# The second attention's queries and keys projected and normed by token, and turned by VectorE and GpSimd's transfers

## The chip, the core and the metric

The kernel runs on one core of a Trainium2 chip. The core's engines have a queue each and run side by side: TensorE (PE: matrix products into PSUM; PEld is its weight load), VectorE (DVE) and ScalarE (ACT) for arithmetic, GpSimd (POOL) and SyncE (SP), which here only issue transfers. ScalarE can issue transfers too. Engines wait for one another by semaphores. The metric is the time of one execution in device microseconds; a lower one is better.

## What is computed

One token block of 256 tokens and width 2048 goes through a pooling mixer with a gated residual, then through a gated DeltaNet layer and a banded attention. All is in float32. The change touches the attention alone (its inputs, cut to what matters):

```
proj = h @ w_in                                  # 256 x 2048 times 2048 x 8192: q, k, v, z
q = rms_norm_2(q by head, q_norm_w)              # 16 heads of 128
k = rms_norm_2(k by head, k_norm_w)
s = q . k * 128**-0.5 + bias                     # bias by distance, band of 9 chunks of 64, causal by chunk
p = softmax(s)
o = (p . v) * silu(z)
out = h + o @ w_out

rms_norm_2(x, w) = x * rsqrt(mean(x*x over the head's 128) + 1e-6) * w
```

## The kernel before

**Projections.** Every large product streams the weights once from DRAM, in 392 slabs of 512 KB (`raw`, four slots). ScalarE rounds a slab to its high part `w_hi` (`hi_parts`), VectorE subtracts for the low part `w_lo` (`lo_parts`), both in eight slots, and TensorE multiplies high by high, high by low and low by high. A group is 512 output columns over all 2048 inputs: eight slabs, one call of `group` or `joined`. ScalarE and VectorE convert slabs from 15 on behind the group's first (`AHEAD = 15`); a slot is free when TensorE has counted up `s_used`. Results go to `acc`, two halves of PSUM used in turn; `s_free` says that VectorE or ScalarE has read one.

**Two orders of a product.** `joined` has the channels on the partitions of the result: it holds a 128×128 piece of weights and streams the operand `b_op` (all 256 tokens, high and low part side by side) past it, 512 columns for the high weights (line 751) and 256 for the low ones (line 753), 64 such pairs a group. It delivers half a group at a time (two units of `acc`). `by_token` (lines 694 to 696) holds the tokens and streams 512 columns of weights, 96 products a group; its result has the tokens on the partitions and channels along the row.

**A round of the attention** takes four heads: groups q, k, v, z (`G_B + 4 i`, ...), then the next four heads, in all four rounds. q, k and z are joined, v is by token. For q and k, ScalarE copies the low part of the result (`low_half`), VectorE adds the high part and multiplies by the root of the token's norm (`evicted_half`), ScalarE squares, the squares are split in a high and a low part (`sq_hi`, `sq_lo`), and TensorE sums them over a head's channels by a product with ones (`split_sums`: four heads, two products each, 128×256), put between two slabs of k and of v. ScalarE then makes the inverse root (`rsqrt`: a logarithm and an exponential, each with a load of its table), VectorE scales by root and norm weight. Since q (`t2`) and k (`t0`) have channels on the partitions, TensorE can multiply them at once: `scores(i)`, put behind slab 6 of v (fillers are called behind a slab of that number, counted from 0).

**Behind the scores**: VectorE adds the bias (`t4`, loaded by GpSimd), masks, takes the maximum; ScalarE exponentiates; VectorE normalises and transposes 32×32 squares inside `p_t` into `p_tt`. The squares themselves change places on a trip through DRAM, issued by ScalarE between its slabs: one write `p_d<-p_tt`, a wait for it, and four reads `p_tt<-p_d` of 32 partitions each, in pieces of 128 B (lines 1604 and 1610). `attended(i)` multiplies with v behind slab 2 of the next q group, or, for the last round, of the first output group.

Every engine's order is the order in which the code is written; no scheduler moves anything. GpSimd's queue is in order too: a transfer behind a wait stays behind it.

## Time and profile before

| | us |
|---|---|
| median of 3 runs (1363.56 to 1366.82) | 1364.05 |
| the profiled execution | 1362.52 |
| its span, first to last instruction | 1360.7 |
| TensorE busy | 1349.9 |
| VectorE busy | 991.2 |
| ScalarE busy | 748.9 |

Busy time is a share of the span and says nothing yet of what waits. A TensorE instruction's row is longer than the distance to the next one, since products overlap; its price is the distance between two starts. The page's slices are 34 us each.

### The profile page before, as it was taken

The numbers are of one execution on the slowest core, as the hardware profiler recorded it, in microseconds if no ns is written. First come the engines' busy times: TensorE is split into PE (matmuls) and PEld (weight loads), VectorE is DVE, ScalarE is ACT, GpSimd is POOL, SyncE is SP. The second block draws the span as 40 slices with busy tenths as digits, with TensorE's granted clock in tenths as the row PEclk, the third lists the DMA queues.
The fourth block names the chain that finished last, engine by engine and source line by source line (L and its number), as shares of the span: only waits on it lengthen the run. The fifth ranks groups of instructions, "written<-read, shape, count | busy, mean of one in ns | idle before, by whom it ended". The sixth has DMA issues, their size and how long they took to land.

```text
span 1360.7 us, 20324 instructions
## 1 busy us (share of the span) xinstructions
PE 1349.9 (99%) x7759; PEld 1149.8 (85%) x7759; DVE 991.2 (73%) x1287; ACT 748.9 (55%) x984; POOL 51.4 (4%) x102
## 2 busy tenths in 40 slices
PE   8999999999999999999999999999999999999999
PEld 4445999988888888888999988888888888888887
DVE  3568989977679999899677677765666566666652
ACT  2214445555766566546788765466476566466431
POOL 0000022000001000010000000000000000000000
PEclk9999999999999999999999999999999999999999
DMA  9999999856476666474645756555755756755752
GB/s 383 414 417 382 346 375 409 302 198 202 159 268 212 223 240 221 170 271 158 201 144 167 225 189 218 192 164 185 206 197 186 203 198 202 201 186 183 222 197 80
DMA packets 105670, 316.30 MB, mean 232 GB/s; under 512 B 33952, under 2 KB 34352, under 8 KB 101104
## 3 DMA queue, kind: packets, MB, share of 16 engines
q1 hardware_dynamic: 67824, 261.30, 55.2%
q0 software_dynamic: 12352, 47.50, 9.7%
q10 hardware_dynamic: 25408, 6.29, 2.2%
q8 instruction: 61, 1.00, 0.3%
q14 instruction: 25, 0.20, 0.0%
HBM read 299.31 MB, written 17.84 MB: 233 GB/s over the span
## 4 chain that ended last, share of the span: by engine, by line
PE 90%; DVE 5%; DMA 3%; issue 1%; SPq 1%; ACT 0%; DVEq 0%; ACTq 0%
PE acc L751 40%; PE acc L753 20%; PE misc L776 3%; PE acc L776 3%; PE misc L1006 3%; PE acc L695 2%; PE acc L694 2%; PE acc L696 2%; DVE w_lo L1665 2%; PE acc L683 2%; PE acc L685 2%; PE acc L686 2%; DMA mod_ring<-mod_w 2%; DMA u_ring<-weights 1%; PE misc L686 1%; PE misc L685 1%
## 5 line engine op out<-in xcount | busy, mean ns | idle before, releaser
L751 PE MATMUL acc<-b_op,w_hi 128*128 128x512 f32 x1792 | 633.3, 398 | 2.1 <-DVE vo L1709 2.1
L1665 DVE TENSOR_TENSOR w_lo<-raw,w_hi 128x1024 fp32r<-128x1024 f32 x392 | 469.8, 1221 | 192.0 <-ACT w_hi L1177 188.1
L1177 ACT ACTIVATE w_hi<-raw 128x1024 fp32r<-128x1024 f32 x392 | 403.7, 1053 | 265.9 <-DMA raw<-weights 116.3
L753 PE MATMUL acc<-b_op,w_lo 128*128 128x256 f32 x1792 | 500.9, 280 | 0.0
L751 PEld LDWEIGHTS acc<-b_op,w_hi 128*128 128x128 f32 x1792 | 336.6, 188 | 80.0 <-DVE vo L1709 2.4
L753 PEld LDWEIGHTS acc<-b_op,w_lo 128*128 128x128 f32 x1792 | 338.2, 189 | 0.3
L751 PE MATMUL acc<-a_op,w_hi 128*128 128x512 f32 x760 | 266.7, 396 | 0.0
L753 PE MATMUL acc<-a_op,w_lo 128*128 128x256 f32 x760 | 212.5, 280 | 0.0
L751 PEld LDWEIGHTS acc<-a_op,w_hi 128*128 128x128 f32 x760 | 142.6, 188 | 33.5 <-DVEq L2132 0.2
L753 PEld LDWEIGHTS acc<-a_op,w_lo 128*128 128x128 f32 x760 | 143.5, 189 | 0.1
L1635 DVE CUSTOM_DVE_ANT_0 mod_ring<-mod_ring,silu_b,vecs 128x2048 f32<-128x2048 f32 x26 | 61.1, 2350 | 46.5 <-DMA mod_ring<-mod_w 46.5
L776 PE MATMUL acc<-u_ring,vo 128*128 128x512 f32 x128 | 57.9, 596 | 4.3 <-ACT vo L1210 2.6
L776 PE MATMUL misc<-u_ring,vo 128*128 128x512 f32 x128 | 57.5, 592 | 0.0
L776 PEld LDWEIGHTS acc<-u_ring,vo 128*128 128x128 f32 x128 | 23.9, 190 | 35.8 <-issue 30.1
L694 PE MATMUL acc<-w_hi,b_op 128*128 128x512 f32 x128 | 50.2, 392 | 0.0
L695 PE MATMUL acc<-w_lo,b_op 128*128 128x512 f32 x128 | 49.9, 390 | 0.0
L696 PE MATMUL acc<-w_hi,b_op 128*128 128x512 f32 x128 | 49.9, 390 | 0.0
L776 PEld LDWEIGHTS misc<-u_ring,vo 128*128 128x128 f32 x128 | 24.3, 190 | 30.1 <-issue 29.9
L1210 ACT ACTIVATE vo<-xres,modv 128x256 f32<-128x256 f32 x16 | 8.1, 508 | 63.8 <-DVE modv L1635 63.8
L1941 DVE SCALAR_TENSOR_TENSOR t<-t,vecs,t 128x255 f32<-128x255 f32 (+2 forms) x96 | 38.9, 478 | 1.9 <-ACT t L1349 1.9
L1006 PE MATMUL misc<-t,t 128*128 128x128 f32 x320 | 38.4, 275 | 0.0
L1006 PEld LDWEIGHTS misc<-t,t 128*128 128x128 f32 x320 | 37.1, 192 | 0.9 <-issue 0.2
(275 smaller groups left out, 1675.1 us busy)
## 6 DMA issues: line engine op xcount, KB each, us to landing
raw<-weights SPq DMA_DIRECT2D x392, 512.0 KB, 4.4
mod_ring<-mod_w SPq DMA_DIRECT2D x26, 1024.0 KB, 12.7
u_ring<-weights SPq DMA_DIRECT2D x32, 512.0 KB, 11.9
gate_ring<-weights POOLq DMA_DIRECT2D x30, 512.0 KB, 8.6
mod_late<-mod_w SPq DMA_DIRECT2D x6, 1024.0 KB, 7.8
p_d<-p_tt ACTq DMA_DIRECT2D x4, 768.0 KB, 3.5
p_tt<-p_d ACTq DMA_DIRECT2D x16, 192.0 KB, 8.0
xres<-x_t SPq DMA_DIRECT2D x4, 512.0 KB, 16.1
```

The lines of the kernel that those rows point to most:

```text
L685: nc.tensor.matmul(to, wh[:, ch], xl, start=False, stop=False, skip_group_check=True)
L686: last = nc.tensor.matmul(to, wl[:, ch], xh, start=False, stop=end and m % 2 == 1, skip_group_check=True)
L694: nc.tensor.matmul(to, xh[:, t], wh, start=kt == 0, stop=False)
L695: nc.tensor.matmul(to, xh[:, t], wl, start=False, stop=False)
L696: last = nc.tensor.matmul(to, xl[:, t], wh, start=False, stop=end)
L751: nc.tensor.matmul(to, w_hi[:, slot, ch], op[:, kt], start=kt == 0, stop=False, skip_group_check=True)
L753: last = nc.tensor.matmul(to[:, 0:T], w_lo[:, slot, ch], op[:, kt, 0:T], start=False, stop=kt == KT - 1, skip_group_check=True)
L776: last = nc.tensor.matmul(bank(2 * j + half), vo[:, kt, half * P:(half + 1) * P], u_ring[:, 2 * (kt % 4) + j // 2, j % 2 * GC:(j % 2 + 1) ...
L1006: last = nc.tensor.matmul(misc[:, k:k + P], tile_of(lhs, half, h), tile_of(rhs, half, h), start=True, stop=True)
L1177: nc.scalar.activation(w_hi[:, m.c % HL_SLOTS], raw[:, q.c % RAW_SLOTS], ACT.Copy).then_inc(own.up(s_hi), 1)
L1635: nc.vector.tensor_tensor_reduce(out=tile, in0=tile, in1=weight, scale=1.0, scalar=start, op0=ALU.mult, op1=ALU.add, accum_out=out).then_i ...
L1665: nc.vector.tensor_tensor(w_lo[:, slot], raw[:, q.c % RAW_SLOTS], w_hi[:, slot].bitcast(F32), ALU.subtract).then_inc(own.up(s_lo), 1)
```

## The change

- q and k are projected by token, as v. The stream of weights is laid out for that (`slabs(m, [q, k, v])`). A round now has five units of `acc` in place of seven.
- Head by head, ScalarE squares the result straight from `acc` with an accumulated sum along the row (`head_squares`), then takes logarithm and exponential of 128×8 numbers. The token's own root is not multiplied in; instead the epsilon is divided by its square (`eps_tok`). VectorE scales head by head with root and norm weight (`head_rows`, loaded once by GpSimd) and transposes 32×32 squares.
- `split_sums` and the splitting of the squares are gone.
- The squares of q, of k and of the probabilities change places by `turned`, on GpSimd's queue: four writes to DRAM in pieces of 512 B, a wait, four reads in pieces of 128 B. ScalarE issues no transfers any more.
- The scores wait for the transfers of q and k (`s_head_t`) and stand behind the last slab of v (slab 7); the attended products stand behind slab 3.

```diff
@@ gpsimd
+            pool.dma_start(head_rows[:], rows_d.to_broadcast([P, 2 * P])).then_inc(s_rows, 16)
...
+            def turned(tile, through, ready, n, written, done):
+
+                pool.wait_ge(ready, n)
+                for a in range(4):
+                    rows = tile[32 * a:32 * a + 32].rearrange("p (n c) -> p n c", c=P)
+                    pool.dma_start(through[:, :, a], rows).then_inc(written, 16)
+                pool.wait_ge(written, 64 * n)
+                for b in range(4):
+                    squares_of = through.rearrange("x n a c -> x (n a) c")[:, :, 32 * b:32 * b + 32]
+                    pool.dma_start(tile[32 * b:32 * b + 32].rearrange("p (k t) -> p k t", t=32), squares_of
+                                   ).then_inc(done, 16)
+
+            pool.wait_ge(s_x1, 5)
+            pool.wait_ge(s_bx, 16)
+            bias_rows(0)
+            for i in range(4):
+                for k, tile in enumerate((t2[:], t0[:, 0:BATCH * T])):
+                    turned(tile, head_d[k], s_head_32, 2 * i + k + 1, s_head_d, s_head_t)
+                if i < 3:
+                    pool.wait_ge(s_biased, i + 1)
+                    bias_rows(i + 1)
+                turned(p_tt[:], p_d, s_turned, i + 1, s_p_d, s_p_tt)
@@ tensor
             def scores(i):
 
-                pe.wait_ge(s_bn, turn(2, i, 2).v)
+                pe.wait_ge(s_head_t, turn(128, i, 128).v)
...
-            joined(G_B, b_op, ready=lambda kt: O_AO + kt + 1, fillers={3: last_sums_b, 6: root_by_token},
-                   order=SPLIT)
+            tokens(G_B, ready=lambda kt: O_AO + kt + 1, fillers={3: last_sums_b, 6: root_by_token})
             for i in range(4):
+                g = G_B + 4 * i
                 if i:
-                    joined(G_B + 4 * i, b_op, fillers={2: lambda: attended(i - 1)})
-                key_value_gate(i)
+                    tokens(g, fillers={3: lambda: attended(i - 1)})
+                tokens(g + 1)
+                tokens(g + 2, fillers={7: lambda: scores(i)})
+                joined(g + 3, b_op)
@@ scalar
+            def head_squares(par, power):
+
+                for half in range(2):
+                    for h in range(BATCH):
+                        k = half * GC + h * P
+                        nc.scalar.activation(squares_b[:, k:k + P], acc[:, par, k:k + P], ACT.Square,
+                                             accum_out=head_sums[:, h, half:half + 1]
+                                             ).then_inc(own.up(s_sq2), 1)
+                act.wait_ge(*own.last())
+                act.wait_ge(s_etok, 1)
+                for half in range(2):
+                    nc.scalar.activation(head_roots[:, :, half], head_sums[:, :, half], ACT.Ln,
+                                         bias=eps_tok[:, half:half + 1], scale=1.0 / P).then_inc(own.up(s_act), 1)
+                act.wait_ge(*own.last())
+                nc.scalar.activation(head_roots[:], head_roots[:], ACT.Exp, bias=power, scale=-0.5
+                                     ).then_inc(own.up(s_rinv), 1)
...
-                act.wait_ge(s_turned, Num(1, i, 1).v)
-                act.dma_start(p_d, p_tt[:]).then_inc(s_p_d, 16)
-                hi_parts(n + 4, 3)
-                act.wait_ge(s_p_d, Num(16, i, 16).v)
-                for b in range(4):
-                    of = bass.AP(tensor=p_d.tensor, offset=p_d.offset + 32 * b,
-                                 ap=[[PAIRS, 32], [P, PAIRS // P], [32 * PAIRS, 4], [1, 32]])
-                    act.dma_start(p_tt[32 * b:32 * b + 32].rearrange("p (n a t) -> p n a t", a=4, t=32), of
-                                  ).then_inc(s_p_tt, 16)
-                hi_parts(n + 7, 1)
+                hi_parts(n + 4, 4)
@@ vector
-                    evicted_half(g, 1, r1, s_qs)
-                    dve.wait_ge(s_sqh, Num(1 + k, i, 2).v)
-                    nc.vector.tensor_tensor(sq_lo[:], t1[:, 0:4 * T], sq_hi[:].bitcast(F32), ALU.subtract
-                                            ).then_inc(own.up(s_sql), 1)
...
                     dve.wait_ge(s_rinv, Num(5 + k, i, 2).v)
...
-                    scaled(out[:, 0:4 * T], src[:, 0:4 * T], vecs[:, w:w + 1], t3[:], done=s_bn)
+                    for half in range(2):
+                        for h in range(BATCH):
+                            at_ = h * T + half * P
+                            scaled(t3[:, at_:at_ + P], acc[:, unit_of(g) % 2, half * GC + h * P:half * GC + (h + 1) * P],
+                                   head_roots[:, h, half:half + 1], head_rows[:, k * P:(k + 1) * P])
+                    dve.wait_ge(*own.last())
+                    dve.sem_inc(own.also(s_free), 1)
+                    if i:
+                        dve.wait_ge(s_score, i)
+                    nc.vector.transpose(out[:, 0:BATCH * T], t3[:]).then_inc(own.up(s_head_32), 1)
+                    lo_parts(n, SLABS)
```

ScalarE in the first round, from the end of the key group to the value group, before (`t_57` is `t1`, `t_59` is `t3`, `small` the constants):

```order
L1202 ACTIVATE k_s<-acc 128x512 [waits s_used]
L1573 ACTIVATE t_57<-k_s 128x1024 [waits s_qs,s_bn]
L1575 ACTIVATE sq_hi<-t_57 128x1024 [waits s_sq2]
...
L1195 ACT_TABLE_LOAD
L1195 ACTIVATE t_59<-misc,small 128x1024 [waits s_nrm]
L1197 ACT_TABLE_LOAD
L1197 ACTIVATE t_59<-t_59 128x1024 [waits s_act]
...
L1588 ACTIVATE v_n<-acc,r_tok 128x512 [waits s_rtok,s_used]
```

and now:

```order
L1579 ACTIVATE squares_b,head_sums<-acc 128x128 [waits s_head_32,s_used]
L1579 ACTIVATE squares_b,head_sums<-acc 128x128 x7
L1585 ACT_TABLE_LOAD [waits s_etok]
L1585 ACTIVATE head_roots<-head_sums,eps_tok 128x4 [waits s_sq2]
L1585 ACTIVATE head_roots<-head_sums,eps_tok 128x4
L1588 ACT_TABLE_LOAD
L1588 ACTIVATE head_roots<-head_roots 128x8 [waits s_act]
...
L1606 ACTIVATE v_n<-acc,r_tok 128x512 [waits s_rtok,s_used]
```

The wait for TensorE's sums (`s_nrm`) is gone; the squares, roots and both table loads now stand in one piece behind the group's end.

GpSimd in the first two rounds, before (`t_60` is `t4`):

```order
L665 DMA xres<-x_d 128x4096 [waits s_solve_pe]
L672 DMA t_60<-bias_x 128x1024 [waits s_bx,s_x1]
L672 DMA t_60<-bias_x 128x1024 [waits s_biased] x3
```

and now (`t_58` is q, `t_56` is k; 256x1x128 are 256 pieces of 128 numbers, 32x32x32 are 1024 pieces of 32):

```order
L673 DMA t_60<-bias_x 128x1024
L680 DMA head_d<-t_58 256x1x128 x4
L684 DMA t_58<-head_d 32x32x32 x4
L680 DMA head_d<-t_56 256x1x128 x4
L684 DMA t_56<-head_d 32x32x32 x4
L673 DMA t_60<-bias_x 128x1024
L680 DMA p_d<-p_tt 384x1x128 x4
L684 DMA p_tt<-p_d 32x48x32 x4
```

Where GpSimd issued one transfer a round, it now issues 25, each trip's reads behind the landing of its writes.

TensorE around the scores of the first round, before:

```order
L695 MATMUL acc<-w_lo,b_op 128x512
L696 MATMUL acc<-w_hi,b_op 128x512
L1113 MATMUL misc<-t_56,t_58 128x256
L1115 MATMUL misc<-t_56,t_58 128x128
...
L694 MATMUL acc<-w_hi,b_op 128x512
...
L751 MATMUL acc<-b_op,w_hi 128x512
L753 MATMUL acc<-b_op,w_lo 128x256
```

and now:

```order
L719 MATMUL acc<-w_lo,b_op 128x512
L720 MATMUL acc<-w_hi,b_op 128x512
L1127 MATMUL misc<-t_56,t_58 128x256
L1129 MATMUL misc<-t_56,t_58 128x128
...
L775 MATMUL acc<-b_op,w_hi 128x512
L777 MATMUL acc<-b_op,w_lo 128x256
```

One slab of v (12 products) stood between the scores and the gate group z; now the scores are followed by z at once.

## Rows read from the trace of the kernel before

**Rows 1.** The page: TensorE's share, and its granted clock in 40 slices.

```profile
PE 1349.9 (99%) x7759; PEld 1149.8 (85%) x7759; DVE 991.2 (73%) x1287; ACT 748.9 (55%) x984; POOL 51.4 (4%) x102
...
PEclk9999999999999999999999999999999999999999
```

**Rows 2.** TensorE's waits (total us, times, longest), first and last of four.

```profile
PE acc L776 <- ACT vo L1210: 2.6, 2, 1.4
...
PE misc L820 <- DVE r L1763: 1.2, 1, 1.2
```

**Rows 3.** TensorE's instructions by time: start us, us, line, out<-in, shapes.

```profile
940.21 0.29 PE L928 MATMUL misc<-sq_hi,ones_r 128*128 128x256 f32 x1
...
941.17 0.39 PE L694 MATMUL acc<-w_hi,b_op 128*128 128x512 f32 x1
...
949.36 0.59 PE L1113 MATMUL misc<-t,t 128*128 128x256 f32 x2
...
951.89 0.48 PE L694 MATMUL acc<-w_hi,b_op 128*128 128x512 f32 x1
...
954.71 0.39 PE L751 MATMUL acc<-b_op,w_hi 128*128 128x512 f32 x1
...
985.79 0.38 PE L1125 MATMUL misc<-p_tt,v_n 128*128 128x128 f32 x2
...
988.39 0.47 PE L751 MATMUL acc<-b_op,w_hi 128*128 128x512 f32 x1
...
1013.44 0.28 PE L928 MATMUL misc<-sq_hi,ones_r 128*128 128x256 f32 x1
...
1045.52 0.59 PE L1113 MATMUL misc<-t,t 128*128 128x256 f32 x2
```

**Rows 4.** ScalarE by time: a table load, the value eviction, exponentials of 128 columns.

```profile
938.83 1.28 ACT L1195 ACT_TABLE_LOAD   x1
...
954.91 1.27 ACT L1588 ACTIVATE v_n<-acc,r_tok 128x512 f32<-128x512 f32 x2 [4.24 <-PE acc L696]
...
961.10 0.39 ACT L1597 ACTIVATE p_t<-p_t,row_max 128x128 f32<-128x128 f32 x1
961.40 0.19 ACT L1597 ACTIVATION_READ_ACCUMULATOR p_t<-p_t,row_max 128x1 f32 x1
961.49 0.39 ACT L1597 ACTIVATE p_t<-p_t,row_max 128x128 f32<-128x128 f32 x1
```

**Rows 5.** VectorE: scalings and transposes, by time, and one group (busy, mean ns).

```profile
565.73 2.69 DVE L1699 SCALAR_TENSOR_TENSOR l_t<-misc,beta,dec_t 128x256 f32<-128x256 f32 x8
...
L2098 DVE STREAM_TRANSPOSE blk<-l_c 128x1024 f32<-128x1024 f32 x1 | 2.1, 2114 | 0.0
...
966.58 1.78 DVE L2284 STREAM_TRANSPOSE p_tt<-p_t 128x1536 f32<-128x1536 f32 x1
```

**Rows 6.** GpSimd's issues by line: count, busy us, mean ns, idle before them.

```profile
L587 POOL DMA_DIRECT2D gate_ring<-weights x30 | 15.8, 528 | 199.5 <-PE acc L776 76.8 <-DVE t L1699 53.9 <-DVE gate_half L1635 41.7
...
L661 POOL DMA_DIRECT2D bias_x<-bias x1 | 1.1, 1068 | 0.0
```

**Rows 7.** DMA issues: count, KB each, median us from issue to landing.

```profile
p_tt<-p_d ACTq DMA_DIRECT2D x16, 192.0 KB, 8.0
...
l_d<-l_t POOLq DMA_DIRECT2D x4, 512.0 KB, 3.0
...
bias_x<-bias POOLq DMA_DIRECT2D x1, 2048.0 KB, 15.5
...
t<-bias_x POOLq DMA_DIRECT2D x4, 512.0 KB, 4.2
```

**Rows 8.** ScalarE's queue by time: the four reads of the first round.

```profile
971.95 10.30 ACTq L1610 DMA_DIRECT2D p_tt<-p_d  x4
```

**Rows 9.** Busy time by stretch; the last columns are PEclk, DMA share, GB/s.

```profile
882.90:1265.80 382.90, 382.90 (x2129) 332.52 (x2128) 241.05 (x243) 230.23 (x289) 1.58 (x3) 1.00 0.61 193
974.00:984.00 10.00, 10.00 (x58) 8.67 (x57) 0.87 (x2) 1.62 (x3) 0.00 (x0) 1.00 0.92 215
```

More of the change, by code:

```diff
@@ L165, in low_of @@
     i, k = divmod(g - G_B, 4)
-    return 2 * (G_AOUT - G_A) + 6 * i + (0, 2, None, 4)[k] + h + 1
+    return 2 * (G_AOUT - G_A) + 2 * i + h + 1
 def first_half(g):
-    return slab_of(Num(g)).c + (7 if g in (G_WOUT, G_A, G_AOUT, G_B, G_BOUT) else 4)
+    return slab_of(Num(g)).c + (7 if g in (G_WOUT, G_A, G_AOUT, G_BOUT) else 4)
 def slab_of(g):
@@ L207, in mod_before, with program @@
     return max(k for k in range(i) if MOD_SLOT[k] == MOD_SLOT[i])
-def program(nc, weights, mod_w, x_t, c_d, vecs_d, consts_d, window_d, w_ab_d, bias_d, out_d):
+def program(nc, weights, mod_w, x_t, c_d, vecs_d, consts_d, window_d, w_ab_d, bias_d, rows_d, out_d):
     ctx = ExitStack()
@@ L348, in half_to @@
             if g >= G_B:
-                return half_of((t0, k_s, None, t1)[(g - G_B) % 4], h)
+                return half_of(t1, h)
             if c < 8:
@@ L359, in program @@
         x_d = nc.dram_tensor("x_d", (P, KT, T), F32).ap()
-        p_d = nc.dram_tensor("p_d", (P, PAIRS), F32).ap()
+        p_d = nc.dram_tensor("p_d", (32, PAIRS // P, 4, P), F32).ap()
+        head_d = [nc.dram_tensor(f"head{k}_d", (32, 2 * BATCH, 4, P), F32).ap() for k in range(2)]
         query_d = nc.dram_tensor("query_d", (P, HEADS * T), F32).ap()
@@ L920, in last_out_sums @@
                 last.then_inc(s_nrm, 1)
-            def split_sums(n):
-                pe.wait_ge(s_ones, 1)
-                pe.wait_ge(s_sql, n.v)
-                for h in range(BATCH):
-                    out, of = misc[:, h * T:(h + 1) * T], slice(h * T, (h + 1) * T)
-                    nc.tensor.matmul(out, ones_r[:], sq_hi[:, of], start=True, stop=False)
-                    last = nc.tensor.matmul(out, ones_r[:], sq_lo[:, of], start=False, stop=True)
-                last.then_inc(s_nrm, 1)
             def key_products(i, q, done):
@@ L1131, in attended, with tokens @@
                 last.then_inc(s_pv, 1)
-            def key_value_gate(i):
-                g = G_B + 4 * i + 1
-                joined(g, b_op, fillers={3: lambda: split_sums(turn(1, i, 2))})
-                u = unit_of(g + 1)
-                group(Num(u - 1), slab_of(Num(g + 1)), u % 2, 0, b_hi, b_lo, products=by_token, fillers={
-                    3: lambda: split_sums(turn(2, i, 2)), 6: lambda: scores(i)})
-                joined(g + 2, b_op)
-            joined(G_B, b_op, ready=lambda kt: O_AO + kt + 1, fillers={3: last_sums_b, 6: root_by_token},
-                   order=SPLIT)
+            def tokens(g, **more):
+                u = unit_of(g)
+                group(Num(u - 1), slab_of(Num(g)), u % 2, 0, b_hi, b_lo, products=by_token, **more)
+            tokens(G_B, ready=lambda kt: O_AO + kt + 1, fillers={3: last_sums_b, 6: root_by_token})
             for i in range(4):
+                g = G_B + 4 * i
                 if i:
-                    joined(G_B + 4 * i, b_op, fillers={2: lambda: attended(i - 1)})
-                key_value_gate(i)
+                    tokens(g, fillers={3: lambda: attended(i - 1)})
+                tokens(g + 1)
+                tokens(g + 2, fillers={7: lambda: scores(i)})
+                joined(g + 3, b_op)
             for j in range(4):
                 joined(G_BOUT + j, a_op, ready=None if j else lambda kt: O_B + kt // 4 + 1,
-                       fillers=None if j else {2: lambda: attended(3)}, order=PLAIN if j else SPLIT)
+                       fillers=None if j else {3: lambda: attended(3)}, order=PLAIN if j else SPLIT)
             last_slab()
@@ L2360, in build_stream @@
         q, k, v, z = (D * part + GC * j for part in range(4))
-        b += [joined_slabs(m, q, PLAIN if j else SPLIT), joined_slabs(m, k), slabs(m, [v]), joined_slabs(m, z)]
+        b += [slabs(m, [q, k, v]), joined_slabs(m, z)]
     rest = np.concatenate([g, grp, joined_stage(i["pool_w_out"][0], quarters), joined_stage(a, order_a),
@@ L2419 @@
         "bias": rel[:, ::-1],
+        "rows": np.concatenate([i["b_q_norm_w_2"], i["b_k_norm_w_2"]], axis=1),
     }
```

78 lines of the change are left out of this document (31 added, 47 removed).

## The prediction

> **What bounds the kernel now.** I read four views, in this order. The page first: TensorE is busy 99% of the span, and its granted clock is full, the 2.4 GHz level, from the first slice to the last [rows 1]. Then TensorE's waits: four groups in the whole span, the largest a few microseconds, and none after 880 us, so in the whole second attention nothing is ever waited for [rows 2]. Third, TensorE's instructions by time, to price its own work. Last, ScalarE, VectorE, GpSimd and the DMA issues, to price the new chain beside it. A kernel of this kind gets faster by exactly what TensorE no longer does, and slower by every microsecond for which it is made to wait. The second attention lasts from 882.9 to 1265.8 us, 382.9 us, four rounds of 96.16 us (scores at 949.36, again at 1045.52) [rows 3, 9].
>
> **TensorE's own work.** Removed: eight blocks of sums of squares. One block is 941.17 − 940.21 = 0.96 us [rows 3], so 8 × 0.96 = 7.7 us. Changed: eight groups (queries and keys, four times) go from joined to by-token order. Both orders stream the same columns (64 × 768 = 96 × 512). By token, the 36 matmuls from 941.17 to 949.36 take 8.19 us, 0.2275 each, so a group of 96 is 21.8 us. Joined, 88 pairs take 985.79 − 954.71 = 31.08 us (0.353 each, 22.6 a group) and the 72 pairs behind the attended products take 1013.44 − 988.39 = 25.05 us (0.348, 22.3 a group) [rows 3]. A converted group is thus worth 0.3 to 0.8 us. The slower pace runs from the scores to the attended products; some pace like it will stay there, so I take 0.4: 3.3 us. Scores and attended products keep their shapes. Sum: −11.0 us, between −10.0 and −14.0 (all eight groups at 0.8).
>
> **The chain to the scores.** Today the key chain has three quarters of the value group before it. Now it starts when the key group ends (call this E) and the scores stand behind the value group's last slab, at E + 21.8. What lies between:
> - TensorE to ScalarE 0.2 (954.71 to 954.91). Eight squares with an accumulated sum of 128 columns: the exponentials of that width follow each other by 961.49 − 961.10 = 0.39, so 3.1. Then two activations on 4 columns and one on 8, about 0.2 each (the shortest ScalarE row there, an accumulator read, takes 0.19), and a table load of 1.28 before the logarithm and one before the exponential, as today [rows 4]. Together 6.5.
> - VectorE: eight scalings of 128×128. Eight of width 256 and 128 mixed take 2.69, so 2.3. The transpose has 1024 columns: 1.78 × 1024/1536 = 1.2; the other 1024-column transposes take 2.1, but they permute, so 1.2 is the nearer one [rows 5]. With semaphores the first GpSimd transfer can be issued at E + 10.4 (bounds 9.9 and 11.9).
> - So the round trip of the keys has 11.4 us. The queries' trip starts 21.8 us earlier and is out of the way if it takes under 21.8.
>
> **The round trip itself**, nowhere in the trace of before in this form. It is four writes of 256 pieces of 512 B, a wait, then four reads of 1024 pieces of 128 B. GpSimd issues a DMA of 128 pieces in 0.53 us and the one of 16×128 = 2048 pieces (bias_x) in 1.07 [rows 6]: (1.07 − 0.53)/1920 = 0.3 ns a piece. The issue alone is then 4 × 0.6 for the writes and 4 × 0.8 = 3.2 for the reads. Writes: the last is issued at 1.8; a GpSimd write of 512 KB lands in 3.0, a quarter of it hardly earlier than 2.5, so they have landed after 4.3 to 5.0. Reads: GpSimd's plain 512 KB read lands in 4.2 [rows 7], a floor of about 5 with the pieces; the same kind of read from ScalarE's queue took 10.3 us to issue for 6144 pieces, 1.7 ns a piece, with the DMA engines 92% busy from 974 to 984 [rows 8, 9]; with about 2 for the last landing (estimate) 12.4, so 4096 pieces take 12.4 × 2/3 = 8.3 at that pace. Round trip: 9.3 to 13.3 us, against a room of 11.4. I take 11.5, about the middle, since the engines' share in this stretch leaves room (0.61) but the weights are no longer held back by a blocked ScalarE. That is late by 0.1; with some scatter on a wait that can't be negative I put 0.3 a round, in all **+1.2 us**. Bounds of this term: 0, and 1.9 + 1.5 (the late start above) = 3.4 a round, 13.6 in all.
>
> **The probabilities' trip.** Now on GpSimd behind the next bias rows (one more issue of 0.53, waited for by nobody until the next round). From the end of the scores (951.89) to the end of the transpose (966.58 + 1.78) are 16.5 us [rows 3, 5]; scores that come one slab later find ScalarE's slab of that moment already done, about 2 less, 14.5. The trip has 6144 pieces: writes 5, reads at most 12.4, so it is ready at 31.9 after the scores. The attended products now stand behind 64 pairs and four slabs by token, 22.6 + 10.9 = 33.5. Slack 1.6: hidden, and 0.4 late in the bad corner (16.5 instead of 14.5). Take 0.
>
> **What else moves.** ScalarE loses its DMA issues with the 10.3 us block [rows 8], the copies, the large squares, logarithms and exponentials; VectorE loses eight half evictions and the subtractions. None is waited for, so I count nothing. Converted weights reach seven slabs (19 us) ahead; the two engines now spend 6.5 and 10 us in a row at a group's end, covered by that. The fourth attended products sit one slab later in the first output group; their operand is needed two slabs (5.5 us) behind, and the multiply, the copy and the subtraction take about 1.2 + 1.1 + 1.2 + semaphores, 4 us: covered by 1.5. The small load of norm rows on GpSimd is 0.53 before the a/b weights, hidden.
>
> **Sum.** 1362.5 (the profiled execution, span 1360.7) − 11.0 + 1.2 = 1352.7. The median of before, 1364.05, stands 1.5 above that execution; the comparison is by medians, so **1354.3**.
>
> Two rules of the Trainium skill. [Rows 6] show thirty GpSimd issues at 528 ns each, with VectorE working beside them. "SBUF — State Buffer", section "SBUF: two separate sides", warns that DMAs issued by GpSimd starve for descriptors while VectorE holds the shared port in a two-port mode; that speaks against this change and is rival D. "DMA: Bandwidth & Descriptors", section "Anatomy of one DMA — SWDGE (gpsimd) path", gives about 2.0 us fixed plus bytes/436e3 and calls descriptor generation small; by it a trip would be about 8 us, the term above 0 and the sum 1353.1. No run here shows that for 128 B pieces.
>
> **Rivals.**
> A, the forecast: the keys' trip fits or is late by up to 1.4 us a round: 1351 to 1358.6. For it: the 1.07 us row. 0.58.
> B, contention: the 128 B reads share the engines with weights that no longer pause. A trip of 13.5 to 15 us is 2.1 to 3.6 late; at 2.8 a round, 11.2 us, the gain is gone: 1364.3. For it: 92% busy in the only stretch with such pieces [rows 9]. 0.17.
> C, slower: GpSimd writes descriptors for short pieces no faster than ScalarE's queue did. The decisive point is about 1.2 ns a piece, where issue and landing fill the 11.4. At 1.7 the writes take 4 × 0.96 + 2.3 = 6.1, the reads 4 × 2.26 + 1.5 = 10.5: 16.6, late by 5.2. The probabilities: 4 × 1.18 + 2.3 + 4 × 3.1 + 1.5 = 21 from 14.5 is 35.5, late by 2.0. Four rounds: 28.8, giving 1354.3 − 1.2 + 28.8 = 1382. Against it: the bias_x row. For it: that row's pieces are 1 KB, run from DRAM to DRAM, and landed only after 15.5 us, 7.6 ns a piece [rows 6, 7]; at that price TensorE would wait about 28 us for each key trip alone. 0.20, most of it near 1382.
> D, slower, as a mechanism here: each issue waits for the end of a VectorE instruction (w_lo, 1.2 us, or a transpose). Eight issues at 0.6 on average add 4.9 to the keys' trip (late by 5.0) and 3.3 net to the probabilities': 33 us, 1386. Against it: the 528 ns row. 0.05.
> That the change doesn't do what it says: the sums are gone from TensorE's order, so that part holds for certain.
>
> **Chances.** Under 0.3% (4.1 us) a measurement can't tell this kernel from no change. Faster by more: A, 0.58. Within: B, 0.17. Slower: C and D, 0.25. The likeliest alone is 1351 to 1359. The range runs from 1350.5 (no wait, and the converted groups at their best) to 1383, which takes in B and most of C; about 0.05 lies below and 0.13 above.
>
> **What would show it.** In the profile after: no sums of squares in the second attention and about 372 us of TensorE work there; the GpSimd issue of a 1024-piece read near 0.8 us (A), near 2.3 (C), or scattered by up to 1.2 (D); from the end of the key group to the first write about 10.4 us; from that write to the last landing 11.5; TensorE's wait at the scores at most 1.4 us a round, and none at the attended products. I am wrong if the scores' wait is over 2 us a round, whatever the cause, or if TensorE's pace by token or joined differs from 0.2275 and 0.35 us.

## The result, and the profile after

| | before | after |
|---|---|---|
| median, us | 1363.80 (1363.19 to 1366.82, 4 runs) | 1387.76 (1382.96 to 1388.51, 4 runs) |
| span of the profiled execution | 1360.7 | 1385.0 |
| TensorE busy | 1349.9 | 1350.2 |

The changed kernel is slower: 1.0164 times the time of before, 95% interval 1.0147 to 1.018. The forecast was 1354.3, in a range of 1350.5 to 1383: a gain was forecast and a loss was measured, and the time lies above the range. Medians here and below are of undisturbed executions; one of the ten of e7_late_only took 1661.35 us and is left out.

TensorE is as busy as before, although 10.5 us of its work are gone (the balance below), and the idle part of its span grew from 10.8 to 34.8 us. The page of after, to be read against [rows 1]:

```profile
PE 1350.2 (97%) x7439; PEld 1138.1 (82%) x7439; DVE 979.1 (71%) x1313; ACT 730.6 (53%) x1088; POOL 120.1 (9%) x199
...
PEclk9999999999999999999999999999999999999999
...
head_d<-t POOLq DMA_DIRECT2D x32, 128.0 KB, 4.3
t<-head_d POOLq DMA_DIRECT2D x32, 128.0 KB, 5.8
```

TensorE's waits (total us, times, longest), against [rows 2]. Nothing was waited for in the second attention before; now the first row alone is 22.1 us:

```profile
PE misc L1127 <- DMA t<-head_d: 22.1, 4, 6.0
...
PE misc L1139 <- DMA p_tt<-p_d: 2.1, 1, 2.1
```

TensorE's instructions around the scores of the first round (start us, us, line, shapes), against [rows 3]:

```profile
949.61 0.39 PE L720 MATMUL acc<-w_hi,b_op 128*128 128x512 f32 x1
955.97 1.22 PE L1127 MATMUL misc<-t,t 128*128 128x256 f32 x2 [5.97 <-DMA t<-head_d]
956.99 0.64 PE L1129 MATMUL misc<-t,t 128*128 128x128 f32 x2
957.41 1.06 PE L1127 MATMUL misc<-t,t 128*128 128x256 f32 x2
...
961.12 0.77 PE L775 MATMUL acc<-b_op,w_hi 128*128 128x512 f32 x1
```

Two things stand in these rows. The wait is 5.97 us. And the scores themselves take 961.12 − 955.97 = 5.15 us, where they took 951.89 − 949.36 = 2.53 before [rows 3]: the same products, twice as long. Busy time by stretch tells why (columns as in [rows 9]; the last three numbers are the granted clock, the DMA share and GB/s):

```profile
939.00:949.50 10.50, 10.50 (x48) 8.71 (x47) 6.83 (x7) 3.19 (x4) 5.01 (x8) 1.00 0.90 282
949.80:955.90 6.10, 0.20 (x1) 0.00 (x0) 1.60 (x2) 2.96 (x4) 0.00 (x0) 0.95 0.97 257
956.00:961.10 5.10, 5.10 (x16) 4.38 (x17) 0.00 (x0) 0.00 (x0) 0.00 (x0) 0.50 0.29 116
```

The granted clock is 1.00 until the wait and 0.50, the 1.2 GHz level, when the products return. The page's PEclk line can't show it, since a stretch of 5 us is lost in a slice of 34. The DMA engines are 90 to 97% busy up to the end of the wait.

GpSimd's issues in that round, the keys' trip:

```profile
938.63 2.39 POOL L680 DMA_DIRECT2D head_d<-t  x4 [11.88 <-DVE t L2268]
946.12 0.79 POOL L684 DMA_DIRECT2D t<-head_d  x1 [5.10 <-DMA head_d<-t]
947.10 2.35 POOL L684 DMA_DIRECT2D t<-head_d  x3 [0.18 <-issue]
```

The first write is issued at 938.63, the first read at 946.12 (writes' stage 7.5 us), and the scores start at 955.97 (reads' stage 9.8): a trip of 17.3 us against the 11.5 of the forecast. ScalarE squares the keys from 929.25 on, TensorE having finished them at 928.0 (the value group's end less its 21.8 us), so 10.6 us lie between the key group's end and the first write, against 10.4 forecast. ScalarE had waited for a weight slab right ahead of them:

```profile
928.29 1.06 ACT L1189 ACTIVATE w_hi<-raw 128x1024 fp32r<-128x1024 f32 x1 [0.94 <-DMA raw<-weights]
929.25 0.26 ACT L1579 ACTIVATE squares_b<-acc 128x128 f32<-128x128 f32 x1
```

**The balance.** The last experiment below computes the same with the granted clock at 1.00 through the whole second attention and TensorE 1339.4 us busy. So the work taken from TensorE is 1349.9 − 1339.4 = 10.5 us, and the low clock put back 1350.2 − 1339.4 = 10.8, about 2.7 for each wait. Span: −10.5 + 10.8 + 24.0 of new idle time = +24.3, the difference of the two spans. Of the 24.0, the scores' waits are 22.1 and the attended products' 2.1.

### The profile page after: what moved, and what is told of

It is laid out like the page before. It is cut to its first block, busy times and chain, and to the rows that moved or that the text cites. A ratio compares the mean times of both kernels' runs of the same rounds, so it can differ in the third digit from the quotient of the medians.

```text
span 1385.0 us, 19890 instructions
## 1 busy us (share of the span) xinstructions
PE 1350.2 (97%) x7439; PEld 1138.1 (82%) x7439; DVE 979.1 (71%) x1313; ACT 730.6 (53%) x1088; POOL 120.1 (9%) x199
## 3 DMA queue, kind: packets, MB, share of 16 engines
q0 software_dynamic: 17520, 62.32, 14.5%
## 4 chain that ended last, share of the span: by engine, by line
PE 66%; DMA 14%; DVE 11%; ACT 3%; issue 2%; POOL 2%; SPq 1%; POOLq 0%; DVEq 0%; ACTq 0%
PE acc L775 28%; PE acc L777 14%; DMA raw<-weights 4%; PE acc L718 4%; PE acc L720 4%; PE acc L719 4%; DVE w_lo L1673 3%; PE misc L1020 3%; DMA mod_ring<-mod_w 2%; DMA t<-head_d 2%; PE misc L800 2%; PE acc L800 2%; DMA head_d<-t 2%; DMA p_tt<-p_d 1%; DMA gate_ring<-weights 1%
## 5 line engine op out<-in xcount | busy, mean ns | idle before, releaser
L775 PE MATMUL acc<-b_op,w_hi 128*128 128x512 f32 x1280 | 454.3, 399 | 2.1 <-DVE vo L1717 2.1
L777 PE MATMUL acc<-b_op,w_lo 128*128 128x256 f32 x1280 | 357.8, 280 | 0.0
L775 PEld LDWEIGHTS acc<-b_op,w_hi 128*128 128x128 f32 x1280 | 240.7, 188 | 57.5 <-DVE vo L1717 2.4
L777 PEld LDWEIGHTS acc<-b_op,w_lo 128*128 128x128 f32 x1280 | 241.9, 189 | 0.1
L718 PE MATMUL acc<-w_hi,b_op 128*128 128x512 f32 x384 | 150.0, 391 | 0.0
L720 PE MATMUL acc<-w_hi,b_op 128*128 128x512 f32 x384 | 149.5, 389 | 0.0
L719 PE MATMUL acc<-w_lo,b_op 128*128 128x512 f32 x384 | 149.4, 389 | 0.0
L720 PEld LDWEIGHTS acc<-w_hi,b_op 128*128 128x128 f32 x384 | 72.1, 188 | 15.2
L718 PEld LDWEIGHTS acc<-w_hi,b_op 128*128 128x128 f32 x384 | 72.1, 188 | 14.8
L719 PEld LDWEIGHTS acc<-w_lo,b_op 128*128 128x128 f32 x384 | 72.1, 188 | 14.7
L1707 DVE SCALAR_TENSOR_TENSOR t<-acc,head_roots,head_rows 128x128 f32<-128x128 f32 x64 | 17.3, 343 | 40.2 <-ACT head_roots L1588 40.2
## 6 DMA issues: line engine op xcount, KB each, us to landing
u_ring<-weights SPq DMA_DIRECT2D x32, 512.0 KB, 12.2
```

Source lines behind the costliest of these rows:

```text
L718: nc.tensor.matmul(to, xh[:, t], wh, start=kt == 0, stop=False)
L719: nc.tensor.matmul(to, xh[:, t], wl, start=False, stop=False)
L720: last = nc.tensor.matmul(to, xl[:, t], wh, start=False, stop=end)
L775: nc.tensor.matmul(to, w_hi[:, slot, ch], op[:, kt], start=kt == 0, stop=False, skip_group_check=True)
L777: last = nc.tensor.matmul(to[:, 0:T], w_lo[:, slot, ch], op[:, kt, 0:T], start=False, stop=kt == KT - 1, skip_group_check=True)
L1707: nc.vector.scalar_tensor_tensor(out=out, in0=src, scalar=scalar, in1=row, op0=ALU.mult, op1=ALU.mult).then_inc(own.up(done or s_dve), 1)
```

## The experiments

The theory after the result: the trip is late by 5 to 6 us a round because its bytes share the DMA engines with the weights, and each wait costs 2.7 us more by the clock. Rivals: the pieces cost it, the trip is that long by itself, or the order by token is to blame.

| run | median us | to before (95%) | wait at scores | at attended |
|---|---|---|---|---|
| changed kernel | 1387.76 | 1.0164 (1.0147 to 1.018) | 22.1 | 2.1 |
| e1_warm | 1381.95 | 1.0135 (1.0114 to 1.0156) | 0.5 | 3.7 |
| e2_no_trip | 1355.89 | 0.9938 (0.9919 to 0.9957) | 0 | 3.1 |
| e3_long_pieces | 1384.7 | 1.0152 (1.0127 to 1.0176) | 18.9 | 2.4 |
| e4_plain_write | 1374.58 | 1.0083 (1.0062 to 1.0105) | 12.5 | 1.3 |
| e5_half_slabs | 1361.55 | 0.9977 (0.9961 to 0.9994) | 7.3 | 2.3 |
| e6_late_plain | 1369.73 | 1.004 (1.0024 to 1.0056) | 0 | 11.0 |
| e7_late_only | 1371.76 | 1.0046 (1.003 to 1.0061) | 2.4 | 5.0 |
| e8_late_six | 1366.43 | 1.0019 (1.0007 to 1.0031) | 8.2 | 0.7 |
| e9_thin_slabs | 1354.44 | 0.9932 (0.9911 to 0.9952) | 1.1 | 1.9 |
| e10_squares_first | 1390.79 | 1.0172 (1.0143 to 1.0202) | 19.7 | 8.8 |
| e11_late_squares | 1357.36 | 0.995 (0.9934 to 0.9966) | 1.9 | 0.6 |

The medians of before beside them lay between 1363.3 and 1364.5 us. The waits are totals over four rounds, from one profiled execution each.

### The clock: TensorE kept busy through the wait

```diff
+                for _ in range(12):
+                    nc.tensor.matmul(misc[:, 1536:1536 + T], ones, consts[:, C_ONE:C_ONE + T], start=True, stop=True)
                 pe.wait_ge(s_head_t, turn(128, i, 128).v)
```

> The changed kernel, with 12 more fp32 products of 128x256 on TensorE in its order, right ahead of the wait at the scores of each round; nothing reads their results. In the trace of the changed kernel that wait is about 6 us and after each of them the granted clock is 0.5, the 1.2 GHz level, for 6.8 us, in which the scores take 4.6 to 5.2 us where they took 2.5 in the kernel before. Theory (the wait has a second price, the clock that falls behind an idle stretch): the products fill most of the wait (12 at 0.59 us or less, 3.5 to 7 us), the granted clock stays 1.0 through the scores, the scores take 2.5 us, and about 2.6 us a round come back: 1377 to 1379 against 1387.8. Rival (the slow scores have another cause, or what fills the wait delays the scores as much): 1387, within 2 us of the changed kernel, or more if the products outlast the wait.

TensorE in the first round of that run:

```profile
951.56 5.34 PE L1125 MATMUL misc<-consts 128*128 128x256 f32 x24
956.91 0.70 PE L1129 MATMUL misc<-t,t 128*128 128x256 f32 x2
...
959.55 0.47 PE L775 MATMUL acc<-b_op,w_hi 128*128 128x512 f32 x1
```

The scores take 959.55 − 956.91 = 2.64 us and the clock of the stretch from 939 to 956 us is 1.00: the slow scores were the clock's doing. The profiled execution gained 9 us of span; the median gained less than I wrote, 5.8 us, or 4 by the ratios, with 1.6 us more waited for at the attended products; 1381.95 lies above the 1377 to 1379 of the theory and below the rival's 1387. The useless products take 5.35 us a round, so this is a test and no remedy.

### TensorE's own work: no trips of q and k

```diff
-                for k, tile in enumerate((t2[:], t0[:, 0:BATCH * T])):
-                    turned(tile, head_d[k], s_head_32, 2 * i + k + 1, s_head_d, s_head_t)
...
-                pe.wait_ge(s_head_t, turn(128, i, 128).v)
+                pe.wait_ge(s_head_32, turn(2, i, 2).v)
```

> The changed kernel without GpSimd's trips of the queries and keys, eight in all; VectorE's transposes of 32x32 squares stay, and the scores wait for those alone. It leaves out the exchange of the squares among each other, so its scores are of other numbers. Theory (TensorE's own work did shrink by 11.0 us, and the whole loss is the trips and what their wait brings with it): no wait at the scores, the granted clock 1.0 throughout, 1363.8 - 11.0 = 1353, within 2 us. Rival (the order by token, or the evictions beside it, costs part of the loss too): 1356 or more, with new waits or a slower pace of TensorE's products in the trace.

1355.89, 7.4 us below before; with the 3.1 us that it waited at the attended products, the work saved is the 10.5 of the balance. That is above the theory's 1351 to 1355 and just under the rival's 1356, so neither fits as it stood. The order by token costs TensorE nothing that was not counted: the scores are not waited for and run at full pace, and the loss of the changed kernel is the trips and what their waits bring. What the theory left out is the third trip, that of the probabilities, which is still there and is waited for in every round, up to 1.5 us. In the kernel with TensorE kept busy it is the same (first and third round):

```profile
993.38 0.46 PE L1141 MATMUL misc<-p_tt,v_n 128*128 128x128 f32 x2 [0.50 <-DMA p_tt<-p_d]
...
1191.97 0.46 PE L1141 MATMUL misc<-p_tt,v_n 128*128 128x128 f32 x2 [1.15 <-DMA p_tt<-p_d]
```

### What makes the trip long: pieces, form of the write, weights

```diff
+                    if done is s_head_t:
+                        rows = tile[32 * b:32 * b + 32].rearrange("p (n c) -> p n c", c=P)
+                        pool.dma_start(rows, through[:, :, b]).then_inc(done, 16)
+                        continue
```

> The changed kernel with the reads of the queries' and keys' trips in pieces of 512 B in place of 128 B: as many DMAs and bytes, a quarter of the pieces. The squares come back where they were, so it leaves out their exchange, as before this its scores are of other numbers. In the changed kernel the trip of the keys takes 17 us from its first write issued, 7.2 of them up to the first read's issue, and four read issues take 3.13 us. Theory (the reads' price is in their pieces): the reads' stage falls from 9.5 us to about 5.5, the wait at the scores from 6 to about 2 us, 1365 to 1377. Rival (bytes, the landing's fixed part and the weights beside them set it): four read issues fall to about 2.4 us, the reads' stage stays over 8 us, and the time is within 4 us of 1387.8.

```diff
-                for a in range(4):
-                    rows = tile[32 * a:32 * a + 32].rearrange("p (n c) -> p n c", c=P)
-                    pool.dma_start(through[:, :, a], rows).then_inc(written, 16)
-                pool.wait_ge(written, 64 * n)
+                pool.dma_start(through, tile).then_inc(written, 16)
+                pool.wait_ge(written, 16 * n)
```

> The changed kernel with the writes of every trip as one DMA of plain rows (4 or 6 KB from each of 128 partitions) in place of four DMAs of 512 B pieces; the reads, still in 128 B pieces, do the whole exchange; the result is computed in full. In the changed kernel the writes' stage, from the first write's issue to the first read's, takes 7.2 us, 2.3 of them issues. Theory (four issues and four landings one behind the other are the cost of that stage): it falls to about 4.5 us, the wait at the scores to about 3 us, 1367 if the granted clock stays 1.0 there and 1377 if it falls. Rival (the bytes share the DMA engines with the weights, whose stretch is over 90% busy, and any form of the write waits for them): the stage stays at 6.5 us or more, and the time is 1383 or more.

```diff
-            slabs_between(56, N_SLABS)
+            slabs_between(56, first)
+            slabs_between(first, last, SLAB_K * GC // 2)
+            slabs_between(last, N_SLABS)
```

(`first` and `last` are the first slabs of the second attention and of the output; the third argument is the number of columns loaded.)

> The changed kernel with the weight slabs of the second attention loaded at half their width (2 KB in place of 4 KB a partition, 128 slabs); the other half of each slab keeps what an earlier one left, so the weights are not the reference's; every instruction that computes stays. In the changed kernel the DMA engines are busy 93% from 939 to 956 us, in which the keys' trip runs, and the trip takes 17 us. Halving the bytes of the trips' pieces' count (512 B reads) left the reads' stage at 9.8 us, and plain writes took the writes' stage from 7.2 to 3.7 us, with the engines at 83%. Theory (both stages wait behind the weights' bytes on the DMA engines): writes' stage 5 us, reads' stage 5 to 7, the wait at the scores under 1.5 us a round, 1355 to 1366. Rival (GpSimd's transfers take this long by themselves, whatever else is moved): the trip stays over 15 us and the time within 4 us of 1387.

The next is the same with 32 columns in place of `SLAB_K * GC // 2` = 512.

> The changed kernel with the weight slabs of the second attention loaded only 32 columns wide (128 B a partition), so next to nothing shares the DMA engines with the trips; the weights are not the reference's. At full width the keys' trip took 17.3 us in the first round (writes' stage 7.6, reads' stage 9.6), at half width 14.3 (6.2 and 8.1), the wait at the scores 1.8 us a round. Theory (the weights' bytes account for the whole distance to the 11.5 us that were forecast): 11 to 12 us, no wait at the scores, about 1353. Rival (a good part is the trip's own: eight landings in two stages, issued one behind the other): 13 us or more, a wait of 1 us or more at the scores in each round, 1357 or more.

The keys' trip of the first round in these four. GpSimd's issues with long pieces and the score that ended the wait, then with the plain write, with half slabs, and with thin slabs:

```profile
940.81 2.29 POOL L680 DMA_DIRECT2D head_d<-t  x4 [13.25 <-DVE t L2272]
947.43 2.32 POOL L685 DMA_DIRECT2D t<-head_d  x4 [4.33 <-DMA head_d<-t]
...
957.28 1.22 PE L1131 MATMUL misc<-t,t 128*128 128x256 f32 x2 [5.80 <-DMA t<-head_d]
```

```profile
940.82 0.58 POOL L678 DMA_DIRECT2D head_d<-t  x1 [16.21 <-DVE t L2268]
944.59 3.92 POOL L684 DMA_DIRECT2D t<-head_d  x4 [3.19 <-DMA head_d<-t]
...
955.07 0.70 PE L1127 MATMUL misc<-t,t 128*128 128x256 f32 x2 [4.19 <-DMA t<-head_d]
```

```profile
938.27 2.39 POOL L684 DMA_DIRECT2D head_d<-t  x4 [11.79 <-DVE t L2272]
944.43 0.79 POOL L688 DMA_DIRECT2D t<-head_d  x1 [3.77 <-DMA head_d<-t]
...
952.57 0.70 PE L1131 MATMUL misc<-t,t 128*128 128x256 f32 x2 [1.96 <-DMA t<-head_d]
```

```profile
938.17 2.39 POOL L684 DMA_DIRECT2D head_d<-t  x4 [12.70 <-DVE t L2272]
943.46 0.79 POOL L688 DMA_DIRECT2D t<-head_d  x1 [2.90 <-DMA head_d<-t]
...
950.34 0.59 PE L1131 MATMUL misc<-t,t 128*128 128x256 f32 x2
```

| | writes' stage | reads' stage | trip | landing of a read, median |
|---|---|---|---|---|
| changed kernel | 7.5 | 9.8 | 17.3 | 5.8 |
| pieces of 512 B | 6.6 | 9.9 | 16.5 | 5.7 |
| one plain write | 3.8 | 10.5 | 14.3 | 7.4 |
| half the weights | 6.2 | 8.1 | 14.3 | 4.4 |
| hardly any weights | 5.3 | at most 6.9 | at most 12.2 | 3.2 |

The pieces fall as a cause: the four issues got 0.8 us shorter (3.13 to 2.32) and the reads' stage not at all.

The plain write halves the writes' stage, as its theory said; it changes the number of transfers and their pieces together, and its reads, from another layout, take 0.98 us each to issue instead of 0.79. Its 1374.58 lies between the theory's two times, 1367 with the clock up and 1377 with it down: behind two of its four waits the first scores ran at full pace to the end, behind the other two they didn't.

The weights are the largest part, 6.3 of the 17.3 us: with them nearly gone, the first round has no wait. There the last read is issued at about 946.0 (the fourth from 943.46, 0.79 apart) and lands 3.2 later: 949.2, a trip of about 11.0 us (estimate from these rows), and the kernel takes 1354.44, against a forecast of 1354.3. Its one wait at the scores, 1.1 us in the last round, falls where the output's weights are already loaded at full width again (the engines' share in that reads' stage is 0.73, in the first round's 0.41).

With half the weights the wait is 1.8 us a round, more than the 1.5 that I had set, so the trip does not shrink in proportion. Narrower slabs take bytes from the DMA engines and from DRAM alike, so these runs don't say which of the two is short. The stretch moves 259 to 274 GB/s, where the page's early slices reach 416, which speaks for the engines, but it isn't shown.

The DMA engines' share of the first round's two stages (writes, reads) with thin slabs, and in the changed kernel:

```profile
938.20:943.40 5.20, 5.20 (x25) 4.30 (x24) 4.86 (x5) 1.47 (x2) 2.22 (x4) 1.00 0.49 110
943.40:950.30 6.90, 6.90 (x32) 5.73 (x31) 4.22 (x4) 2.78 (x3) 3.14 (x4) 1.00 0.41 86
```

```profile
938.60:946.10 7.50, 7.50 (x35) 6.21 (x34) 4.87 (x5) 1.06 (x1) 2.25 (x4) 1.00 0.83 259
946.10:955.90 9.80, 3.90 (x18) 2.89 (x16) 4.26 (x4) 5.39 (x6) 3.14 (x4) 0.97 0.96 274
```

### Cover: scores and attended products later

All five of these compute everything. The first (its two lines that move the scores; the rest is in the text below them):

```diff
-                tokens(g + 2, fillers={7: lambda: scores(i)})
-                joined(g + 3, b_op)
+                tokens(g + 2)
+                joined(g + 3, b_op, fillers={1: lambda: scores(i)})
```

> The whole computation. Plain writes in every trip, as in the run before with that edit alone (writes' stage 3.7 us, the trip 14.2, waits at the scores 12.5 us in four), and the scores put behind slab 1 of the gate group z (5.6 us later), the attended products one slab later too (behind slab 4 of the next query group, and of the first output group); the value's accumulators are read out before the scores' turn, and half of z's evictions moved with it. Theory (the wait is all that stands against the gain of 11 us on TensorE): the wait of 3.1 us a round is covered by 5.6, the granted clock stays 1.0 at the scores, and the time is 1363.3 - 11 = 1352 to 1355, faster than both. Rival (a later score makes the probabilities late by as much, and the value's tiles or z's evictions are now waited for): new waits of 1 to 3 us a round at the attended products or at an accumulator, 1357 to 1366.

Wrong, and by its own arithmetic. Two slabs of z (5.6 us) went ahead of the scores and only one slab by token (2.7) ahead of the attended products, so the cover between them shrank from 33.5 to 30.6. The wait moved there, 2.76 us in the first round, 11.0 in all, and TensorE is 1345.4 us busy, 6.0 above the last kernel, by the low clock behind those waits. So the rival had the place, and 1369.73 is still above its 1366:

```profile
PE misc L1139 <- DMA p_tt<-p_d: 11.0, 4, 3.9
```

> The whole computation, with the changed kernel's trips untouched, and the scores behind slab 2 of z (8.4 us later), the attended products behind slab 6 of the next query group (8.2 us later) and slab 5 of the first output group. Theory (cover is all that lacks, whatever a trip takes): the trip of 17 us against 11.4 + 8.4 of room leaves no wait at the scores; the last attended products have two slabs less than the others, a wait of up to 5 us once, with a stretch at the 1.2 GHz level behind it; 1353 to 1360. Rival (the trips' share of the DMA engines delays the weights themselves): waits for converted weights at the slabs beside the trips, 1360 or more.

Wrong as well, by its rival's mechanism in part. TensorE waited for no converted weights, but once, in the output, for half an accumulator: VectorE read that out (line 1717) behind a conversion for which it had itself idled 3.2 us. The trips stayed long, and the last operand of the output now came late:

```profile
PE misc L1139 <- DMA p_tt<-p_d: 5.0, 3, 2.4
PE acc L775 <- DVE a_op L2309: 3.8, 1, 3.8
...
PE misc L1127 <- DMA t<-head_d: 2.4, 2, 1.6
PE acc L775 <- DVE t L1717: 2.1, 1, 2.1
```

> The whole computation: plain writes, the scores behind slab 1 of z in the first three rounds and behind slab 0 in the last, the attended products behind slab 6 of the next query group (and slab 4 of the first output group). In the run with the scores behind slab 1 and the attended products behind slab 4, no wait was left at the scores, but 11.0 us in four at the attended products: between scores and attended products there were 30.6 us of TensorE work, and the probabilities needed 15.4 from the scores to the first write and 17.4 to 18 for their trip, 33.4 in all. Theory (waits at either end of the exchange are the only loss): 36 us of cover in three rounds and 33.4 in the last leave at most 0.5 us of waits, the granted clock stays 1.0, and 1354 to 1357 follows, 0.5% faster than the kernel before. Rival (the loss moves on once more: gate, converted weights or the last operand are late by then): new waits at the accumulators of together over 4 us, 1360 or more.

Wrong again: its 1354 to 1357 came out as 1366.43. No wait was left in the first two rounds, but 2.1 us in the third and 6.1 in the last, at the scores and not at the accumulators where the rival had put it, and the median stayed 0.2% above before. ScalarE in the last round shows a delay that I had not had on my list (start us, us, what ended the idle time before):

```profile
1214.48 1.06 ACT L1189 ACTIVATE w_hi<-raw 128x1024 fp32r<-128x1024 f32 x1 [3.52 <-DMA raw<-weights]
1215.44 0.26 ACT L1579 ACTIVATE squares_b<-acc 128x128 f32<-128x128 f32 x1
```

The squares stand in ScalarE's queue behind the conversion of a weight slab, and that slab is late because the queries' trip is on the DMA engines with it (share 0.97 from 1202 to 1214.5 us). In e2_no_trip, where that trip is gone, ScalarE waited 0.18 us for the slab at this place:

```profile
1208.62 1.06 ACT L1187 ACTIVATE w_hi<-raw 128x1024 fp32r<-128x1024 f32 x1 [0.18 <-DMA raw<-weights]
```

The chain starts 23.8 us behind the query group's, where TensorE needs 21.8. So I moved one conversion behind the squares, on ScalarE and VectorE, in the changed kernel alone and then on top of this one:

```diff
-                    hi_parts(n, SLABS)
+                    hi_parts(n + (-1 if k else 0), SLABS + (1 if k else -1))
```

> The changed kernel with the squares of the key group one weight slab earlier in ScalarE's order (the slab's two conversions follow the chain, on VectorE as well). In the changed kernel ScalarE converts a slab right ahead of these squares, and where it waits for that slab's DMA (0.94, 1.47 and 0.98 us in the first three rounds) the squares start late: 22.7, 22.3 and 21.8 us behind the query group's squares, where TensorE's group takes 21.8. Theory (the chain starts late because the weights land late): 0.9, 0.5 and 0 us earlier, 1 to 2 us in all with the clock's part, 1384 to 1387. Rival (the chain's end is what counts, and the late slab now stalls something else): no change or slower, 1388 or more.

> The whole computation: the run with the attended products behind slab 6, with the same move of the key group's squares. There the squares started 23.5 us behind the query group's in the first round and 23.8 in the last, 1.7 and 2.0 late, behind a slab that ScalarE waited 2.4 and 3.5 us for, and TensorE waited 8.2 us in two rounds at the scores (6.1 in the last, which has a slab less of cover, and 1.2 GHz behind it). Theory (the late start is part of that wait): 8.2 falls to about 4.5, and the time from 1366.4 by about 4 to 6 us, 1360 to 1363, so faster than the kernel before by at most 0.3%. Rival (the weights' landing moves with the trips whatever the order, and another conversion is late in its place): 1365 or more, or waits for converted weights at an accumulator.

In the changed kernel alone it brings nothing: the waits at the scores fall from 22.1 to 19.7, those at the attended products rise from 2.1 to 8.8, and the interval of its ratio overlaps the changed kernel's. Its rival was right. On top of the later places it is worth 9 us, more than I had put. TensorE's waits and the page of that last kernel:

```profile
PE misc L1127 <- DMA t<-head_d: 1.9, 1, 1.9
...
PE acc L775 <- DVE a_op L2309: 1.1, 1, 1.1
PE misc L1139 <- DMA p_tt<-p_d: 0.6, 1, 0.6
```

```profile
PE 1339.4 (99%) x7439; PEld 1129.8 (83%) x7439; DVE 978.5 (72%) x1313; ACT 726.9 (54%) x1088; POOL 110.4 (8%) x163
```

1357.36 us: 0.995 of before (0.9934 to 0.9966), faster than both kernels. Of the 10.5 us of work saved, 6.5 were had; 3.6 still go into the three waits above. How much of the step from 1366.4 to 1357.4 is the earlier chain itself and how much the changed meeting of trips and weights on the DMA engines, these runs don't tell apart.

## Why the prediction was wrong, point by point

- **TensorE's own work**, −11.0 forecast, −10.5 measured: right.
- **The chain to the first write**, 10.4 us forecast, 10.6 measured in the first round: right, with luck. The squares started 1.25 us behind the key group's end where I had 0.2, and then took 0.25 each where I had 0.39. Its bounds left out that the weights ahead of the squares could come late, up to 2 us in later variants.
- **The issue price**, 0.3 ns a piece from [rows 6]: right. The read's 1024 pieces took 0.79 us to issue, so rival C's mechanism did not happen. By number D (1386) is the nearest and C (1382) the next, but neither for its reason.
- **The round trip**, 11.5 us (bounds 9.3 to 13.3), measured 17.3: this is the step that failed. Its terms were landings of single transfers from [rows 7] and one stretch at 92% share [rows 9]. The number fits a kernel whose weights don't compete (about 11.0 with thin slabs). I had read the mean share of the whole second attention, 0.61 [rows 9], as room "in this stretch"; in the stretch itself the share is 0.83 and 0.96. In the kernel before, the same microseconds have 0.71 and 0.55; the trip with thin slabs, nearly alone, has 0.49 and 0.41. Together that is 1.20 and 0.96: in the writes' stage more than there is, so something had to stretch. Rival B named this mechanism and priced it at 13.5 to 15.
- **The clock**, not in the sum at all: +10.8 us. The forecast, B, C and D all charged a wait at its length; each wait of 5 to 6 us cost about 1.5 times that, once as idle time and once as scores at the 1.2 GHz level. With it, a wait of the size that B priced (2.8 us a round, 1364.3) can cost far more: e4_plain_write waits 3.1 a round and takes 1374.58. The trip alone doesn't decide. It is 14.3 us there and in e5_half_slabs, but the first write goes out 11.9 us behind the key group's end in the one and 9.7 in the other (first rounds); e5_half_slabs waits 1.8 a round, has TensorE 1341.3 us busy, so nearly no low clock, and takes 1361.55. Of the 33.5 us between forecast and median, the waits at the scores are 20.9 (22.1 less the 1.2 in the sum), the clock 10.8, and the wait at the attended products 2.1.
- **The probabilities' trip**, ready at 31.9 us behind the scores (14.5 to the first write, 17.4 for the trip) and hidden with 1.6 to spare, taken at 0: nearly right, and the trip was sized too small here as well. From the scores' end (961.12) to its first write (975.97) are 14.9 us, near the 14.5. The trip took 21.2 us in the last round of the changed kernel (from 1280.12), the only one that TensorE waited for, and 19.1 to 20.0 in e1_warm, against 17.4; it took 17.4 only with the plain write, in e6_late_plain (975.15 to 992.58).

```profile
1301.27 0.46 PE L1139 MATMUL misc<-p_tt,v_n 128*128 128x128 f32 x2 [2.07 <-DMA p_tt<-p_d]
```

So the 1.6 were used up: 2.1 us once in the changed kernel, 3.1 and 3.7 in all four rounds of the two runs without the low clock behind the scores. e6_late_plain, which shortened the cover between scores and attended products, paid 11.0.

- **What moves otherwise**, counted at nothing: right for TensorE, whose other waits stayed those of before.
- **What would show me wrong** was a wait over 2 us a round at the scores. It is 5.5. Rival D would have shown as issues scattered by up to 1.2 us: the sixteen writes of the probabilities lie between 594 and 674 ns.

The profile of before did hold the warning. [Rows 9] have a trip with the engines at 0.92 while ScalarE, blocked by its issues, was holding the weights back. Without that block, more had to be asked of the same engines at once; that is how I read the rows, and no run takes it apart.

## What to carry to other kernels

Price a transfer by the DMA share of the very microseconds in which it will run, with the new transfers added, and not by the mean of the stage; here a landing of 3.2 us became one of 5.8 at shares of 0.83 to 0.96. Where TensorE may come to wait for some microseconds, charge the products behind the wait at the lower clock too. And when a wait is covered by moving the consumer, move every later consumer of the same chain by as much, and look at what stands ahead of the chain's first instruction in its queue.

## What the runs showed of the hardware

- **The clock behind a wait.** In the changed kernel the scores behind the four waits (5.1 to 6.0 us) ran at a granted clock of 0.50 to 0.56. The length of the wait alone doesn't decide: in e4_plain_write the scores behind waits of 2.00 and 3.36 us started at full pace (0.70 us, then 0.60), those behind 2.95 at the low level (1.22, then 1.06), and behind 4.19 only the first pair was fast, as behind 2.25 in the last round of e5_half_slabs:

```profile
1148.80 0.70 PE L1127 MATMUL misc<-t,t 128*128 128x256 f32 x2 [3.36 <-DMA t<-head_d]
...
1246.77 1.22 PE L1127 MATMUL misc<-t,t 128*128 128x256 f32 x2 [2.95 <-DMA t<-head_d]
```

What decides between 2 and 5 us I have not settled. The Trainium skill, "TensorE: Matmul & The Clock Gate", section "HAM oscillation — how this bites in real kernels", describes this: waits for a DMA make the next products start at the low clock. The trace of the changed kernel agrees, with the 0.50 from 956.0 to 961.1 us.

- **Landing by load.** The median landing of the same 128 KB read on GpSimd's queue was 3.2, 4.4 and 5.8 us with weight slabs 32, 512 and 1024 columns wide; of the 128 KB write 2.7, 3.5 and 4.3. The Trainium skill, "DMA: Bandwidth & Descriptors", section "Anatomy of one DMA — SWDGE (gpsimd) path", gives 2.0 us plus bytes/436e3, an estimate of 2.3 for either. The write with hardly any weights is near that; the loaded queue is not, and there the measurement decides.
- **Pieces.** Reads in pieces of 512 B took no less time than in pieces of 128 B: 9.9 and 9.8 us.
